# HGRN2 in a hybrid decoder layer on one core: state carried from tile to tile with decayed keys between chunks, and every projection step of a tile behind the next tile's scores

## The chip, the core and the metric

The kernel runs on one core of a Trainium2 chip. The core has five engines that run side by side, each with its own queue of instructions: TensorE (PE) for matmuls, VectorE (DVE), ScalarE (ACT), GpSimd (POOL), and SyncE (SP), which here only issues transfers. They wait for each other through semaphores. The metric is the time of one execution on the device in microseconds (us); lower is better.

## The reference, cut to what matters

A layer normalizes x (1024 tokens by 1024 channels, float32), projects it with one matrix into the inputs of four mixers (attention with forgetting, "FoX"; a state-space scan, "SSD"; gated linear attention, "GLA"; and HGRN2, "HGRN"), then adds cross-attention and a gated feed-forward part. The change touches HGRN alone. It has 4 heads with keys of 64 and values of 64 channels, and runs causally over time in chunks of 16 tokens:

```
q_dec = q * exp(g_cs)                 # g_cs: cumulated log decay inside the chunk
k_inv = k * exp(-g_cs)
k_end = k * exp(g_cs[:, :, -1:] - g_cs)
att = where(causal, einsum('bnihd,bnjhd->bnhij', q_dec, k_inv), 0.0)
o = einsum('bnhij,bnjhv->bnihv', att, v)
d_state = einsum('bnjhd,bnjhv->bnhdv', k_end, v)
s_in = scan_chunk_states(d_state, exp(g_cs[:, :, -1])[..., None])     # s * g + ds
o = o + einsum('bnihd,bnhdv->bnihv', q_dec, s_in)
```

Every chunk so has its own state s_in, 64 x 64 for a head, and the states follow one from another: 64 chunks in a row.

## The kernel before

All four mixers stand in `mixers_block`, with every engine's program written out by hand; the order of the work is the order of the code. Data lie with channels on the 128 partitions and the 1024 tokens along the row (a "slot"; `data(s)` is a slot, `tile(s, i)` the 128 tokens of tile i). So a pair p of heads fills the partitions, and there are two pairs.

**The projection runs in the gaps of the mixers.** Its unit is a half: one group of 128 columns of w_in against 512 tokens, 8 steps in k with three matmuls each (a high and a low part of both factors, `split_matmuls`, lines 99 to 101), 24 matmuls. ACT makes the high part of a group's weights (`hi`, L449), DVE the low part (`lo`, L759), and ACT copies each finished half out of PSUM (`copy_out`, L461). `fill(s0, s1)` issues single steps on PE, `halves(m0, m1)` whole halves. The table `_HG` says which halves stand beside HGRN: two in each of the four stretches of the preparation (`HG_PREP`), one at each of tiles 0 to 3, none at tiles 4 to 7 (`HG_TILE`).

**Preparation.** For each pair DVE and ACT in turn make the decays over all 1024 tokens (lines 565 to 576 on ACT, 830 to 849 on DVE): q_dec in `data(B + p)`, k_inv in `data(A + 4 + p)`, k_end in `data(B + 2 + p)`. The last one counts `h_prep`; PE, POOL and DVE wait for it before the tiles.

**Tiles.** A tile is 128 tokens, 8 chunks. On PE `hgrn_scores(i)` transposes values and k_end (L1169) and makes the scores of all four heads, k_inv against QX (L1175; QX is q_dec with the other head's rows set to zero, made by POOL, L407). DVE copies the scores through the mask M16, which keeps only what is causal and within one chunk (L856). `hgrn_states(i, p)` makes the eight d_state of each head in one matmul with 512 columns (L1184); for that POOL spreads the values over eight blocks (VX, L414). DVE then forms the eight states of a pair one after another, `S * ED + d_state`, one instruction of 64 x 64 for each head and chunk (L870), 32 for a tile. `hgrn_outputs(i, p)` needs all eight: two matmuls of masked scores with the values (L1196), then eight with 16 columns, each with its own chunk's state (L1199). ACT copies the transposes (L581) and the outputs (L585).

After tile 7 PE waits until every half is copied out and goes on with the norms of FoX (L1120), whose squares ACT makes first (L501).

## Time and profile before

| | |
|---|---|
| median of 3 runs | 1805.25 us (1805.08 to 1807.98) |
| the profiled execution, its own time | 1803.33 us |
| its span, first to last instruction | 1801.6 us |
| PE busy | 1690.7 us, 94% of the span |
| DVE, ACT, POOL busy | 876.9, 666.7, 74.3 us |
| mean granted TensorE clock | 0.974 of full speed |
| preparation, first projection step to first tile | about 137 to 184 us |
| tiles of HGRN | about 184 to 305 us |

Instructions are named by their line, engine and operation, then output and inputs, shapes, count, and time. A float32 matmul leaves two records on PE (a transpose leaves one), so 32 matmuls read as x64. Matmuls overlap: the distance between two starts is the price of one in a row, the duration shown is longer. "PEld" is the load of the factor that stays in the array; its columns are the second number in 128*64. A clock of 1.00 is TensorE's 2.4 GHz, 0.50 its 1.2 GHz.

### The profile page before, as it was taken

Reading aid. Unit: us, or ns where it says so; the run is one execution under the profiler, and the core shown is the slowest. Engines: PE = TensorE matmul, PEld = TensorE weight load, DVE = VectorE, ACT = ScalarE, POOL = GpSimd, SP = SyncE. Lnnn points to the kernel's source line nnn. Section 1 sums busy time; section 2 is a strip of 40 time slices with the busy share of each in tenths; the row PEclk is TensorE's granted clock in tenths of the full one; section 3 lists DMA queues with packets and bytes.
Section 4 is the critical chain, followed back from the end, with each engine's and each line's share of the span. In section 5 each row is a group of like instructions: output and inputs, shape, how many; then the busy total and the mean of one; then the engine's idle time right before and its main releaser. Section 6 shows DMA issues by size and latency. Waiting matters only on the chain.

```text
span 1801.6 us, 20927 instructions
## 1 busy us (share of the span) xinstructions
PE 1690.7 (94%) x8140; PEld 1350.6 (75%) x8140; DVE 876.9 (49%) x1471; ACT 666.7 (37%) x1186; POOL 74.3 (4%) x119
## 2 busy tenths in 40 slices
PE   6999898999887786999999999999999999999997
PEld 5788565666665454878888888888888888888886
DVE  4315576567466564544345325555533455555322
ACT  5224112754522435434343214334333344433321
POOL 2000432000010020000000000000000000000000
PEclk9999898999999898999999999999999999999999
DMA  5121000000020212600001113333222333333222
GB/s 143 47 48 37 23 12 1 24 24 25 24 70 13 70 59 67 243 6 24 1 24 65 36 47 94 94 103 96 72 92 94 118 101 103 113 94 105 88 97 97
DMA packets 166922, 121.32 MB, mean 67 GB/s; under 512 B 23448, under 2 KB 140456, under 8 KB 166824
## 3 DMA queue, kind: packets, MB, share of 16 engines
q1 hardware_dynamic: 165496, 115.53, 21.3%
q10 hardware_dynamic: 1328, 4.46, 0.7%
q8 instruction: 65, 1.06, 0.2%
q14 instruction: 33, 0.27, 0.0%
HBM read 115.77 MB, written 4.19 MB: 67 GB/s over the span
## 4 chain that ended last, share of the span: by engine, by line
PE 59%; DVE 1%; ACT 0%; DMA 0%; issue 0%; DVEq 0%
PE tail_b L99 18%; PE tail_b L100 18%; PE tail_b L101 18%; PE tail_b L2119 2%; PE tail_b L2094 1%; PE tail_b L2083 0%; PE tail_b L2106 0%; PE tail_b L2031 0%; DVE tail_wl L1795 0%; PE tail_b L2154 0%; PE tail_b L2238 0%; DMA tail_wr<-in_w_out 0%; DVE tail_xs L1830 0%; ACT tail_xs L1630 0%; DVE XR L1958 0%
## 5 line engine op out<-in xcount | busy, mean ns | idle before, releaser
L1951 DVE TENSOR_TENSOR ff_wl<-ff_wr,ff_wh 128x512 fp32r<-128x512 f32 (+1 forms) x176 | 168.5, 958 | 329.8 <-ACT ff_wh L1738 329.8
L1738 ACT ACTIVATE ff_wh<-ff_wr 128x512 fp32r<-128x512 f32 (+1 forms) x176 | 149.0, 847 | 377.6 <-PE tail_b L101 377.6
L99 PE MATMUL tail_b<-HH,ff_wh 128*128 128x512 f32 x704 | 273.9, 389 | 0.0
L100 PE MATMUL tail_b<-HL,ff_wh 128*128 128x512 f32 x704 | 273.9, 389 | 0.0
L101 PE MATMUL tail_b<-HH,ff_wl 128*128 128x512 f32 x704 | 273.9, 389 | 0.0
L99 PE MATMUL mix_gb<-HH,mix_wh 128*128 128x512 f32 x432 | 180.2, 417 | 7.7 <-ACT slots L461 3.8
L100 PE MATMUL mix_gb<-HL,mix_wh 128*128 128x512 f32 x432 | 170.7, 395 | 0.0
L101 PE MATMUL mix_gb<-HH,mix_wl 128*128 128x512 f32 x432 | 170.5, 395 | 0.0
L99 PE MATMUL tail_b<-tail_wh,HH 128*128 128x512 f32 x384 | 153.9, 401 | 9.4 <-DVE tail_wl L1795 8.2
L99 PEld LDWEIGHTS tail_b<-HH,ff_wh 128*128 128x128 f32 x704 | 132.2, 188 | 27.6
L101 PEld LDWEIGHTS tail_b<-HH,ff_wl 128*128 128x128 f32 x704 | 132.2, 188 | 27.6
L100 PEld LDWEIGHTS tail_b<-HL,ff_wh 128*128 128x128 f32 x704 | 132.2, 188 | 27.1
L101 PE MATMUL tail_b<-tail_wh,HL 128*128 128x512 f32 x384 | 150.3, 391 | 0.0
L100 PE MATMUL tail_b<-tail_wl,HH 128*128 128x512 f32 x384 | 150.3, 391 | 0.0
L99 PEld LDWEIGHTS mix_gb<-HH,mix_wh 128*128 128x128 f32 x432 | 82.8, 192 | 31.8 <-issue 6.3
L759 DVE TENSOR_TENSOR mix_wl<-mix_wr,mix_wh 128x1024 fp32r<-128x1024 f32 x43 | 53.5, 1246 | 102.9 <-ACT mix_wh L449 102.6
L99 PE MATMUL tail_b<-ff_wh,ff_aha 128*128 128x512 f32 x256 | 100.2, 392 | 0.0
L100 PE MATMUL tail_b<-ff_wl,ff_aha 128*128 128x512 f32 x256 | 99.7, 389 | 0.0
L100 PEld LDWEIGHTS mix_gb<-HL,mix_wh 128*128 128x128 f32 x432 | 82.6, 191 | 18.8 <-issue 2.7
L101 PEld LDWEIGHTS mix_gb<-HH,mix_wl 128*128 128x128 f32 x432 | 82.5, 191 | 17.9
L99 PEld LDWEIGHTS tail_b<-tail_wh,HH 128*128 128x128 f32 x384 | 72.6, 189 | 24.3 <-issue 10.3
L101 PEld LDWEIGHTS tail_b<-tail_wh,HL 128*128 128x128 f32 x384 | 72.5, 189 | 15.6
(315 smaller groups left out, 2586.4 us busy)
## 6 DMA issues: line engine op xcount, KB each, us to landing
ff_wr<-in_ffn_w_up SPq DMA_DIRECT2D x88, 512.0 KB, 3.7
ff_wr<-in_ffn_w_down SPq DMA_DIRECT2D x88, 256.0 KB, 2.8
mix_wr<-in_w_in SPq DMA_DIRECT2D x26, 512.0 KB, 3.6
mix_wr<-in_xa_wkv SPq DMA_DIRECT2D x16, 512.0 KB, 3.6
XR<-in_x SPq DMA_DIRECT2D x8, 512.0 KB, 6.4
tail_wr<-in_w_out SPq DMA_DIRECT2D x16, 256.0 KB, 5.6
XR<-in_x ACTq DMA_DIRECT2D x1, 4096.0 KB, 19.2
tail_wr<-in_xa_wq SPq DMA_DIRECT2D x16, 256.0 KB, 4.4
```

Source lines behind the costliest of these rows:

```text
L99: pe.matmul(out, hi_w, hi_x, start=first, stop=False)
L100: pe.matmul(out, hi_w, lo_x, start=False, stop=False)
L101: return pe.matmul(out, lo_w, hi_x, start=False, stop=last)
L759: dve.tensor_tensor(WL[:, n % PART, :, :], WR[:, n % RAW, :, :], WH[:, n % PART, :, :], ALU.subtract)\
L1738: act.activation(part(FWH[m % FPART], m), part(FWR[m % FRAW], m), ACT.Copy).then_inc(w_hi, 1)
L1951: dve.tensor_tensor(part(FWL[m % FPART], m), part(FWR[m % FRAW], m), part(FWH[m % FPART], m), ALU.subtract)\
L2094: mm = pe.matmul(bank[3 + g][:, hh * N_MEM:(hh + 1) * N_MEM], QT[:, 2 * h + kk, :], ktr(2 * h + kk), start=(kk == 0), stop=(kk == 1))
L2119: mm = pe.matmul(bank3[6 + g][:, j, :], vv(m, d), PT[:, m, d // 2, :], start=(m == 0), stop=(m == 1))
```

## The change

The state is now kept per tile instead of per chunk, and what a chunk owes to earlier chunks of the same tile is computed as scores.

- **Scores.** The product within the chunk stays (now L1229 in the changed kernel). For each chunk a from 1 to 7 and each pair, PE multiplies the keys of chunks 0 to a-1, decayed up to the start of chunk a, by the two heads' queries of chunk a: 16a keys by 2 x 16 queries (L1234), 14 matmuls for a tile. They write where the first product left terms that are not wanted. The mask MC keeps all that is causal.
- **Keys.** DVE makes those keys from k_end and a table DECAY of decays between chunk ends (`hgrn_keys`, L882: for each pair one instruction of 256 elements a partition for a = 1 to 4, KLO, and one of 512 for a = 5 to 8, KHI). KHI's last block, keys decayed to the tile's end, is what is transposed for the state.
- **State.** One matmul of 128 columns for each pair (L1243) and four DVE instructions a tile (`hgrn_update`, L902) instead of 32. POOL's VX (L414 before) is gone.
- **Outputs.** Two matmuls of scores as before and one of 128 columns with the tile's state and QE, queries decayed from the tile's start, which POOL makes (L414 of the changed kernel). Outputs have a bank of their own (M[4]), scores two (M[1], M[5]), tile states two (M[2], M[3]).
- **Preparation.** For each pair DVE has a copy, a scan and a difference over 64 chunk ends, and a difference and a minimum over 512 elements for DECAY; ACT has two more exponentials (128 and 512 elements).
- **Projection.** `_HG` counts in steps: 16 in each stretch of the preparation (two halves, as before), and 4 in each of the eight tiles, all in `HG_B`, behind the outputs of tile i and the scores of tile i+1. `HG_A`, ahead of the outputs, is empty. The sum stays 4 halves.

```diff
-_HG = spread(2 * F0, 2 * S0, [2, 2, 2, 2] + [1, 1, 1, 1, 0, 0, 0, 0])
-HG_PREP, HG_TILE = _HG[:4], _HG[4:]
...
+_HG = spread(2 * F0 * KT, 2 * S0 * KT, [16] * 4 + [0, 4] * NT)
+HG_PREP, (HG_A, HG_B) = _HG[:4], in_two(_HG[4:])
...
-        work = SL[:, W1:W1 + 5, :].rearrange("p a b -> p (a b)")
-        VX = work[:, 0:2048].rearrange("p (h c d) -> p h c d", h=4, c=8)
-        S_HG = work[:, 2048:2048 + 2304].rearrange("p (q c e) -> p q c e", q=2, c=9)
+        work = SL[:, A:A + 4, :].rearrange("p a b -> p (a b)")
+        KLO = [[work[:, 768 * (2 * b + p):768 * (2 * b + p) + 256] for p in range(2)] for b in range(2)]
+        KHI = [[work[:, 768 * (2 * b + p) + 256:768 * (2 * b + p) + 768] for p in range(2)] for b in range(2)]
+        S_HG = [work[:, 3072 + 256 * b:3328 + 256 * b].rearrange("p (q e) -> p q e", q=2) for b in range(2)]
+        QE = [work[:, 3584 + 256 * b:3840 + 256 * b].rearrange("p (q t) -> p q t", q=2) for b in range(2)]
+        DECAY = [data(W1)[:, 512 * p:512 * p + 512] for p in range(2)]
+        EC, EX = [ED[:, p, 0:64] for p in range(2)], [ED[:, p, 64:128] for p in range(2)]
...
+                if i >= 2:
+                    pool.wait_ge(E("h_y"), i - 1)
+                for p in range(2):
+                    pool.tensor_tensor(QE[i % 2][:, p, :].rearrange("p (c j) -> p c j", j=CH_HGRN),
+                                       tile(B + p, i).rearrange("p (c j) -> p c j", j=CH_HGRN),
+                                       EX[p][:, 8 * i:8 * i + 8].unsqueeze(2).to_broadcast([P, 8, CH_HGRN]), ALU.mult)\
+                        .then_inc(E("h_qe"), 1)
...
+                act.wait_ge(E("hg_ends"), p + 1)
+                act.activation(ED[:, p, :], a1[:, 64:192], ACT.Exp).then_inc(E("hg_ed"), 1)
+                act.activation(DECAY[p], DECAY[p], ACT.Exp).then_inc(E("hg_ed"), 1)
+                halves(*begun(HG_PREP[2 * p + 1]))
...
+            hgrn_vk(0)
+            for i in range(NT):
+                if i + 1 < NT:
+                    hgrn_vk(i + 1)
+                new = range(*begun((HG_A[i][0], HG_B[i][1])))
+                act.wait_ge(E("h_y"), i + 1)
+                act.activation(MX[:, 6:8, i * P:(i + 1) * P], M3[4][:, 0:2, :], ACT.Copy).then_inc(E("h_yev"), 1)
+                for m in new:
+                    halves(m, m + 1)
+            act.wait_ge(E("h_yev"), NT)
...
+            dve.wait_ge(E("st_tr"), NT)
...
                 dve.wait_ge(E("hg_ln"), p + 1)
+                if p:
+                    dve.wait_ge(E("hg_ed"), 2 * p)
...
+                dve.wait_ge(E("hg_cum"), p + 1)
+                link(dve.tensor_copy(low, ends16(2)))
+                link(dve.tensor_tensor_scan(cum, SL[:, A + 3, PAD:PAD + 128:2], low, 0.0, ALU.mult, ALU.add))
+                by_tile = cum.rearrange("p (t c) -> p t c", c=8)
+                dve.tensor_tensor(before, cum, low, ALU.subtract).then_inc(E("hg_dif"), 1)
+                dve.tensor_tensor(DECAY[p].rearrange("p (t a b) -> p t a b", a=8, b=8),
+                                  by_tile.unsqueeze(3).to_broadcast([P, NT, 8, 8]),
+                                  by_tile.unsqueeze(2).to_broadcast([P, NT, 8, 8]), ALU.subtract).then_inc(E("hg_dif"), 1)
+                dve.wait_ge(E("hg_dif"), 2 * p + 2)
+                dve.tensor_scalar(DECAY[p], DECAY[p], 0.0, None, ALU.min).then_inc(E("hg_ends"), 1)
                 dve.wait_ge(E("hg_e1"), p + 1)
-                link(dve.tensor_copy(ED[:, p, :], SL[:, A, PAD + CH_HGRN - 1:SW:CH_HGRN]))
...
+            def hgrn_keys(i):
+                if i >= 2:
+                    dve.wait_ge(E("h_att"), i - 1)
+                    dve.wait_ge(E("h_tr"), i - 1)
+                for p in range(2):
+                    k = tile(B + 2 + p, i).rearrange("p (b j) -> p b j", j=CH_HGRN)
+                    decay = DECAY[p][:, 64 * i:64 * i + 64].rearrange("p (a b) -> p a b", b=8)
+                    for buf, a, nb in ((KLO[i % 2][p], 0, 4), (KHI[i % 2][p], 4, 8)):
+                        dve.tensor_tensor(buf.rearrange("p (a b j) -> p a b j", a=4, b=nb),
+                                          k[:, 0:nb, :].unsqueeze(1).to_broadcast([P, 4, nb, CH_HGRN]),
+                                          decay[:, a:a + 4, 0:nb].unsqueeze(3).to_broadcast([P, 4, nb, CH_HGRN]),
+                                          ALU.mult).then_inc(E("h_ka"), 1)
+
...
+                    dve.wait_ge(E("h_y"), i - 1)
+                dve.copy_predicated(ATT[i % 2], MC[:].bitcast(mybir.dt.uint32).unsqueeze(1).to_broadcast([P, 4, P]),
+                                    M3[1 + 4 * (i % 2)]).then_inc(E("h_am"), 1)
+
+            def hgrn_update(i):
+                dve.wait_ge(E("h_ds"), i + 1)
+                if i >= 1:
+                    dve.wait_ge(E("h_s"), 4 * i)
+                    dve.wait_ge(E("h_y"), i)
                 for p in range(2):
...
+                    for hh in range(2):
+                        q, e = slice(64 * hh, 64 * hh + 64), slice(64 * hh, 64 * hh + 64)
+                        dve.scalar_tensor_tensor(S_HG[(i + 1) % 2][q, p, e], S_HG[i % 2][q, p, e],
+                                                 EC[p][q, 8 * i + 7:8 * i + 8], M3[2 + i % 2][q, p, e], ALU.mult, ALU.add)\
+                           .then_inc(E("h_s"), 1)
+
+            hgrn_keys(0)
+            hgrn_keys(1)
+            dve.wait_ge(E("att_zero"), 1)
+            hgrn_mask(0)
+            dve.wait_ge(E("s_zero"), 1)
+            late = range(0)
+            for i in range(NT):
+                if i + 1 < NT:
+                    hgrn_update(i)
+                if i + 2 < NT:
+                    hgrn_keys(i + 2)
+                if i + 1 < NT:
+                    hgrn_mask(i + 1)
+                for m in late:
+                    halves(m, m + 1)
+                late = range(*begun((HG_A[i][0], HG_B[i][1])))
+            for m in late:
+                halves(m, m + 1)
...
+                    pe.transpose(M3[0][:, j, :], tile(B + 4 + j, i), ident)
+                pe.wait_ge(E("h_ka"), 4 * i + 4)
+                for j in range(2):
+                    last = pe.transpose(M3[0][:, 2 + j, :], KHI[i % 2][j][:, 3 * P:4 * P], ident)
+                last.then_inc(E("h_tr"), 1)
+
+            def hgrn_scores(i):
+                pe.wait_ge(E("h_qx"), 2 * i + 2)
                 if i >= 2:
-                    pe.wait_ge(E("h_yev"), i - 1)
-                for j in range(4):
-                    last = pe.transpose(M3[0][:, j, :], tile((B + 4, B + 5, B + 2, B + 3)[j], i), ident)
-                last.then_inc(E("h_tr"), 1)
-                pe.wait_ge(E("h_qx"), 2 * i + 2)
+                    pe.wait_ge(E("h_am"), i - 1)
+                att = M3[1 + 4 * (i % 2)]
+                for p in range(2):
+                    pe.matmul(att[:, 2 * p:2 * p + 2, :], tile(A + 4 + p, i), QX[:, 2 * p:2 * p + 2, :], start=True, stop=True,
+                              skip_group_check=True)
+                    for a in range(1, 8):
+                        keys, q = KLO[i % 2][p][:, 64 * (a - 1):64 * (a - 1) + 16 * a] if a <= 4 else \
+                            KHI[i % 2][p][:, P * (a - 5):P * (a - 5) + 16 * a], slice(16 * a, 16 * a + 16)
+                        mm = pe.matmul(att[0:16 * a, 2 * p:2 * p + 2, q], keys, QX[:, 2 * p:2 * p + 2, q], start=True,
+                                       stop=True, skip_group_check=True)
+                mm.then_inc(E("h_att"), 1)
...
+            def hgrn_states(i):
+                pe.wait_ge(E("h_vk"), i + 1)
+                if i >= 2:
+                    pe.wait_ge(E("h_s"), 4 * (i - 1))
+                for p in range(2):
+                    mm = pe.matmul(M3[2 + i % 2][:, p, :], VK[i % 2][:, 2 + p, :], VK[i % 2][:, p, :], start=True, stop=True)
+                mm.then_inc(E("h_ds"), 1)
+
...
+                vk, yb = VK[i % 2], M3[4]
+                pe.wait_ge(E("h_vk"), i + 1)
+                pe.wait_ge(E("h_am"), i + 1)
+                pe.wait_ge(E("h_qe"), 2 * i + 2)
+                pe.wait_ge(E("s_zero"), 1)
                 if i >= 1:
-                    pe.wait_ge(E("h_am"), i)
+                    pe.wait_ge(E("h_s"), 4 * i)
+                    pe.wait_ge(E("h_yev"), i)
...
+                    for hh in range(2):
+                        pe.matmul(yb[64 * hh:64 * hh + 64, p, :], vk[:, p, 64 * hh:64 * hh + 64], ATT[i % 2][:, 2 * p + hh, :],
+                                  start=True, stop=False, skip_group_check=True)
+                    mm = pe.matmul(yb[:, p, :], S_HG[i % 2][:, p, :], QE[i % 2][:, p, :], start=False, stop=True,
                                    skip_group_check=True)
                 mm.then_inc(E("h_y"), 1)
...
+            hgrn_transposes(0)
             hgrn_scores(0)
-            for p in range(2):
-                hgrn_states(0, p)
             for i in range(NT):
                 if i + 1 < NT:
+                    hgrn_transposes(i + 1)
+                    hgrn_states(i)
+                fill(*HG_A[i])
+                hgrn_outputs(i)
+                if i + 1 < NT:
                     hgrn_scores(i + 1)
-                halves(*HG_TILE[i])
-                for p in range(2):
-                    hgrn_outputs(i, p)
-                    if i + 1 < NT:
-                        hgrn_states(i + 1, p)
+                fill(*HG_B[i])
```

The first place is PE's own row of work for one tile. Here stands what it does before, from the transposes and scores of tile 3 to the first state matmul behind the outputs of tile 2 (gb is the projection, m0 holds transposes and outputs, m1 the scores, m2 to m5 the states; "..." stands for the other projection matmuls of the half):

```order
L1169 MATMUL mix_m0<-ident,slots 128x128 [waits mix_h_yev,mix_h_vk]
L1175 MATMUL mix_m1<-mix_scratch,slots 128x256 [waits mix_h_am,mix_h_qx]
L99 MATMUL mix_gb0<-HH,mix_wh 128x512 [waits mix_g_ev,mix_g_lo]
...
L1196 MATMUL mix_m0<-mix_scratch 64x128 [waits mix_h_vk,mix_h_yev,mix_h_s,mix_h_am]
L1199 MATMUL mix_m0<-slots 128x16 x8
L1184 MATMUL mix_m2<-slots,mix_scratch 128x512 [waits mix_h_s,mix_h_vx]
```

The like stretch of PE after the change, one tile earlier, from the transposes of tile 2 over the outputs of tile 1 and the scores of tile 2 to the first of the 12 projection matmuls:

```order
L1217 MATMUL mix_m0<-ident,slots 128x128 [waits mix_h_vk]
L1220 MATMUL mix_m0<-ident,slots 128x128 [waits mix_h_ka]
L1243 MATMUL mix_m3<-mix_scratch 128x128 [waits mix_h_vk]
L1257 MATMUL mix_m4<-mix_scratch 64x128 [waits mix_s_zero,mix_h_s,mix_h_qe,mix_h_yev,mix_h_am,mix_h_vk]
L1259 MATMUL mix_m4<-slots 128x128
L1229 MATMUL mix_m1<-mix_scratch,slots 128x256 [waits mix_h_am,mix_h_qx]
L1234 MATMUL mix_m1<-mix_scratch,slots 16x2x16
L1234 MATMUL mix_m1<-mix_scratch,slots 32x2x16
...
L1234 MATMUL mix_m1<-mix_scratch,slots 112x2x16
L99 MATMUL mix_gb0<-HH,mix_wh 128x512
```

The scores moved from ahead of the outputs to behind them, the projection from between scores and outputs to the tile's end, and the 512-column state matmuls became one of 128 columns ahead of the outputs.

The second place is DVE at the start of a tile's work, before (tile 1; M16 mask, then the chain of 64 x 64 updates, each with a wait for the one before it on the same head):

```order
L856 COPY_PREDICATED mix_scratch<-mix_m16,mix_m1 128x512 [waits mix_h_att]
L870 SCALAR_TENSOR_TENSOR slots<-slots,mix_ed,mix_m2 64x64 [waits mix_h_y,mix_h_ds]
L870 SCALAR_TENSOR_TENSOR slots<-slots,mix_ed,mix_m3 64x64
L870 SCALAR_TENSOR_TENSOR slots<-slots,mix_ed,mix_m2 64x64 [waits mix_h_s]
L870 SCALAR_TENSOR_TENSOR slots<-slots,mix_ed,mix_m3 64x64 [waits mix_h_s]
```

And DVE after the change, the mask of tile 0, the update of the state over tile 0, the keys of tile 2 and the mask of tile 1:

```order
L891 COPY_PREDICATED mix_scratch<-mix_mc,mix_m1 128x512 [waits mix_h_att,mix_att_zero]
L902 SCALAR_TENSOR_TENSOR slots<-slots,mix_ed,mix_m2 64x64 [waits mix_h_ds,mix_s_zero]
L902 SCALAR_TENSOR_TENSOR slots<-slots,mix_ed,mix_m2 64x64 x3
L882 TENSOR_TENSOR slots<-slots 128x256 [waits mix_h_tr,mix_h_att]
L882 TENSOR_TENSOR slots<-slots 128x512
L891 COPY_PREDICATED mix_scratch<-mix_mc,mix_m5 128x512 [waits mix_h_att]
```

The 32 updates with their waits became four, and four products for keys stand between update and mask (the two more that follow read the same and are left out).

## Rows read from the trace of the kernel before

**Rows 1.** Page, part 1: busy time and share of the span.

```profile
PE 1690.7 (94%) x8140; PEld 1350.6 (75%) x8140; DVE 876.9 (49%) x1471; ACT 666.7 (37%) x1186; POOL 74.3 (4%) x119
```

**Rows 2.** Page, part 4: the chain that ended last.

```profile
PE 59%; DVE 1%; ACT 0%; DMA 0%; issue 0%; DVEq 0%
```

**Rows 3.** Windows: length, then PE, PEld, DVE, ACT, POOL busy, clock, DMA.

```profile
137.00:184.00 47.00, 45.62 (x197) 37.31 (x196) 26.01 (x23) 21.59 (x26) 0.00 (x0) 0.96 0.20 45
184.00:306.00 122.00, 107.62 (x544) 74.91 (x544) 80.53 (x266) 12.56 (x24) 45.49 (x49) 0.90 0.04 9
```

**Rows 4.** Groups by shape, 184 to 306 us: busy, mean ns, idle before.

```profile
L870 DVE SCALAR_TENSOR_TENSOR slots<-slots,mix_ed,mix_m 64x64 f32<-64x64 f32 x256 | 71.7, 280 | 13.0 <-PE mix_m L1184 5.0
L414 POOL TENSOR_TENSOR slots<-mix_scratch,mix_cm 128x512 f32<-128x512 f32 x32 | 34.4, 1105 | 59.5 <-ACT mix_scratch L581 59.5
L1199 PEld LDWEIGHTS mix_m<-slots 128*128 128x128 f32 x256 | 31.5, 200 | 2.9 <-issue 2.9
L407 POOL TENSOR_TENSOR mix_scratch<-slots,mix_hm 128x256 f32<-128x256 f32 x16 | 9.5, 613 | 0.0
L856 DVE COPY_PREDICATED mix_scratch<-mix_m 128x512 f32<-128x512 uint32 x8 | 5.9, 732 | 5.7 <-PE mix_m L1175 5.5
L1196 PEld LDWEIGHTS mix_m<-mix_scratch 128*64 128x64 f32 x64 | 3.5, 139 | 20.7 <-issue 17.1 <-DVE mix_scratch L856 3.6
```

**Rows 5.** Timeline of PE, one tile: start, length, what, idle before; projection left out.

```profile
247.17 0.60 PE L1169 MATMUL mix_m<-ident,slots 128*128 128x128 f32 x4
247.61 1.03 PE L1175 MATMUL mix_m<-mix_scratch,slots 128*128 128x256 f32 x4
...
254.05 0.44 PE L1196 MATMUL mix_m<-mix_scratch 128*64 128x128 f32 x4
254.42 1.96 PE L1199 MATMUL mix_m<-slots 128*128 128x16 f32 x16
256.23 1.96 PE L1184 MATMUL mix_m<-slots,mix_scratch 128*128 128x512 f32 x4
...
262.10 0.60 PE L1169 MATMUL mix_m<-ident,slots 128*128 128x128 f32 x4
```

**Rows 6.** Timeline of PE: two projection matmuls, three starts apart.

```profile
249.17 0.40 PE L99 MATMUL mix_gb<-HH,mix_wh 128*128 128x512 f32 x1
...
249.86 0.40 PE L99 MATMUL mix_gb<-HH,mix_wh 128*128 128x512 f32 x1
```

**Rows 7.** Timeline of PE: first scores, last outputs, first norm of FoX.

```profile
187.23 2.08 PE L1175 MATMUL mix_m<-mix_scratch,slots 128*128 128x256 f32 x4 [2.58 <-POOL mix_scratch L407]
...
301.09 3.60 PE L1199 MATMUL mix_m<-slots 128*128 128x16 f32 x16
307.82 3.71 PE L1120 MATMUL mix_m<-slots,mix_bo 128*128 128x512 f32 x4 [3.14 <-ACT slots L501]
```

**Rows 8.** Timeline of DVE: scan, repeated operand, last of the preparation, low part.

```profile
149.87 2.29 DVE L838 TENSOR_TENSOR_SCAN slots<-slots 128x1024 f32<-128x1024 f32 x1
...
180.37 1.22 DVE L846 TENSOR_TENSOR slots<-slots 128x1024 f32<-128x1024 f32 x1
...
182.72 1.22 DVE L849 TENSOR_TENSOR slots<-slots 128x1024 f32<-128x1024 f32 x1 [1.13 <-ACT slots L576]
...
196.62 1.73 DVE L759 TENSOR_TENSOR mix_wl<-mix_wr,mix_wh 128x1024 fp32r<-128x1024 f32 x1 [6.45 <-ACT mix_wh L449]
```

**Rows 9.** Timeline of ACT in the preparation: two copies of halves.

```profile
154.11 0.57 ACT L461 ACTIVATE XR<-mix_gb 128x512 f32<-128x512 f32 x1
...
166.34 0.60 ACT L461 ACTIVATE XR<-mix_gb 128x512 f32<-128x512 f32 x1 [3.89 <-PE mix_gb L101]
```

**Rows 10.** Timeline of POOL: the four VX products of tile 1.

```profile
195.23 5.03 POOL L414 TENSOR_TENSOR slots<-mix_scratch,mix_cm 128x512 f32<-128x512 f32 x4 [2.91 <-ACT mix_scratch L581]
```

**Rows 11.** Timeline of PE in FoX: 32 records with 64 loaded columns.

```profile
405.42 1.92 PE L1271 MATMUL mix_m<-mix_scratch,slots 128*64 128x128 f32 x32
```

**Rows 12.** Windows of 1 us, columns as in rows 3.

```profile
271.00:272.00 1.00, 1.00 (x2) 0.38 (x2) 0.89 (x4) 0.15 (x1) 0.00 (x0) 0.50 0.00 0
```

More of the change, by code:

```diff
@@ L384, in _ @@
             keep(NEGK[:], ALU.is_ge, 0, [[1, P]], -1, NEG)
-            for m, ch in ((M64, CH_GLA), (M16, CH_HGRN)):
-                v = m[:].rearrange("p (c i) -> p c i", i=ch)
-                keep(m[:], ALU.is_ge, 0, [[1, P]], -1)
-                keep(v, ALU.is_ge, 0, [[-ch, P // ch], [0, ch]], 1)
+            keep(MC[:], ALU.is_ge, 0, [[1, P]], -1)
+            keep(M64[:], ALU.is_ge, 0, [[1, P]], -1)
+            keep(M64[:].rearrange("p (c i) -> p c i", i=CH_GLA), ALU.is_ge, 0, [[-CH_GLA, P // CH_GLA], [0, CH_GLA]], 1)
             for m, n in ((BM, 4), (BO64, 2)):
@@ L393, in _ @@
                 keep(v, ALU.is_ge, w - 1, [[w, n], [0, 64]], -1)
-            for m, n in ((HM4, 4), (HM2, 2), (CM8, 8)):
+            for m, n in ((HM4, 4), (HM2, 2)):
                 w = P // n
@@ L564, in _ @@
             for p in range(2):
-                halves(*HG_PREP[2 * p])
+                halves(*begun(HG_PREP[2 * p]))
                 act.wait_ge(E("hg_abs"), p + 1)
@@ L829, in _ @@
             link(dve.memset(SL[:, A + 3, PAD:SW:CH_HGRN], 0.0))
+            ends16 = lambda j: SL[:, A + j, PAD + CH_HGRN - 1:SW:CH_HGRN]
+            low, cum, before = a1[:, 0:64], a1[:, 64:128], a1[:, 128:192]
+            dve.wait_ge(E("st_tr"), NT)
             for p in range(2):
@@ L849, in _ @@
                 dve.tensor_tensor(z, z, a2, ALU.mult).then_inc(E("h_prep"), 1)
-            dve.wait_ge(E("att_zero"), 1)
-            dve.wait_ge(E("s_zero"), 1)
-            for i in range(NT):
+            dve.wait_ge(E("h_prep"), 2)
+            dve.wait_ge(E("hg_ed"), 4)
+            def hgrn_keys(i):
[10 more added lines that the diff above has]
+                                          ALU.mult).then_inc(E("h_ka"), 1)
@@ L853, in _, with hgrn_mask @@
+            def hgrn_mask(i):
                 dve.wait_ge(E("h_att"), i + 1)
                 if i >= 2:
[L855 to L873 removed]
```

87 lines of the change are left out of this document (14 added, 73 removed).

## The prediction

> **What bounds the kernel now.** First the page: PE is busy for 94% of the span [rows 1] and the chain that ended last is PE with hardly anything else [rows 2]. So only what PE does, or waits for, counts. Then the windows: the preparation of HGRN takes 47 us, of which PE works 45.6, and its tiles take 122 us, of which PE works 107.6 at a granted clock of 0.90 [rows 3]. Four halves of the projection stand in the tiles. One matmul of it costs 0.69 / 3 = 0.23 us [rows 6], a half 24 x 0.23 = 5.5, so 22 us of the 122 are projection. The other 100 are HGRN.
>
> The groups of that stretch [rows 4] show who makes PE wait: DVE updates states for 71.7 us, 256 instructions of 0.28 us one behind the other, and POOL spreads values for 34.4 us. The timeline of one tile [rows 5] shows PE's own bill, 262.10 - 247.17 = 14.9 us: transposes 0.44, scores and a half 6.44 (so 0.9 for the scores), outputs 0.37 + 1.81 twice, and what is left, 1.85 twice, states. Sixteen records with 16 moving columns cost 1.81 us, 0.113 each, though they move next to nothing; the load of 128 columns sets that price. A tile without a half costs PE 9.4 us, and DVE 32 x 0.28 + 0.73 = 9.7. Both bound the stage, taking turns.
>
> The stage runs from the first scores at 187.2 us to the last output at 301.09 + 3.60 = 304.7, and 3.1 us later the norms begin at 307.8 [rows 7].
>
> **The change part by part.** I add up where PE will stand, on the clock of the profiled execution.
>
> *Preparation.* For each pair DVE gets, behind the scan that ends at 152.2 [rows 8], three operations on 64 elements and two on 512. The nearest rows are 0.28 (64 x 64) and 0.73 us (512) [rows 4], so at most 2.3: done by 154.5. ACT, which began its copy at 154.1 [rows 9], now first has exponentials of 128 and 512 elements, some 0.3 and 0.6 (its 512-element copy takes 0.6 [rows 9]). So that copy slips by 0.8 (if short operations overlap) to 1.3 us; I take 1.0. The slip of the first pair is swallowed, since ACT later waits 3.9 us for PE anyway [rows 9]. That of the second moves the end of the preparation from 182.72 + 1.22 = 183.9 [rows 8] to 184.9. PE needs the slipped copy at about 166.3 - 2 x 5.5 = 155.4 and gets it at 155.7, so it may lose some tenths, twice; PE has 1.4 us to spare in this stretch (45.6 of 47 [rows 3]), which hides them. DVE's new wait on the transposes of the gates delays nothing: ACT takes up its result only after the next half.
>
> *First tile.* DVE then makes keys(0): two operations of 512 elements and two of 256. By 0.73 for 512 and 1.22 for 1024 [rows 4, 8] a 256 costs at most 0.5, so 2.5 us, until 187.4. POOL meanwhile zeroes less and makes QX (1.2 a pair of products [rows 4]). The trace shows that DVE and POOL collide: the low part of the weights took 1.73 us beside POOL's products, and those took 5.03 for four instead of the 34.4 / 32 x 4 = 4.3 of the mean [rows 8, 10]. By 0.5 us for a clash, one or two of them give 188.0 with bounds of 187.0 and 188.8; the first scores start at 188.3 with the last two transposes.
>
> The Trainium skill has a rule for this, and it speaks against the change ("SBUF — State Buffer", Who interferes with whom): a DVE instruction with two SBUF inputs and a GpSimd instruction that reads SBUF exclude each other for the whole instruction. The new keys are just that kind. By that rule in full the start would be 1 us later than by the row and each tile of DVE up to 2 us longer, which DVE has to spare (below); the sum by the rule would be 1 us higher.
>
> *Small score matmuls.* This is the unknown price: 14 matmuls a tile, 28 records, with 16 to 112 loaded columns and 32 moving. The nearest rows: 0.113 for 128 columns with 16 moving [rows 5], and 1.92 / 32 = 0.06 for 64 columns with 128 moving [rows 11]. The loads themselves read 200 ns for 128 columns and 139 for 64 [rows 4], so columns count. I take 0.06 up to 64 columns and 0.113 x columns / 128 above: for a pair 2 x (4 x 0.06 + 0.071 + 0.085 + 0.099) = 1.0, for a tile 2.0 us. The bounds are 448 / 128 x 0.113 x 4 = 1.6 and 28 x 0.113 = 3.2.
>
> The rule of the Trainium skill ("TensorE: Matmul & The Clock Gate", LDWEIGHTS (loading the stationary operand)) is that a load's time goes with its columns, at 1.2 columns a ns. That would make the 28 loads 1.5 us instead of my 2.0, and the whole kernel 4 us faster than my sum. The rows of the loads agree in direction, 139 ns for 64 columns against 200 for 128.
>
> *A tile in the steady state.* Transposes 0.44; two state matmuls of 128 columns, four records at 0.113, 0.45; outputs 2 x 0.37 [rows 5] + 4 x 0.113 = 1.19; scores 0.9 + 2.0 = 2.9; projection 12 x 0.23 = 2.76. Sum 7.74 us, against 14.9 with a half and 9.4 without. Is anything else as long? DVE: four updates 1.1, keys 2.5, mask 0.73, a low part (1.23 to 1.73) every second tile: 5.2, or 6 with clashes. POOL: 1.2 for QX and at most 1.2 for QE. ACT: two copies of 0.6 and every second tile a copy and a high part. The waits: mask(i) is ready 0.9 us after scores(i), and the outputs that need it stand 2.76 + 0.44 + 0.45 = 3.65 us behind, so the moved projection covers it. Without that cover PE would wait 0.9 - 0.9 = 0, behind transposes and states alone, plus some tenths of latency. The keys of tile i+2 are done 3.6 us after states(i), PE asks for them after 6.8. So PE runs through.
>
> *Sum.* Scores(0) run at the half clock, since PE stands idle ahead of them, as it did before (2.58 us right ahead of 187.2 [rows 7]): 2 x 2.9 = 5.8, from 188.3 to 194.1. Mask 0.9: 195.0. Outputs(0), scores(1), projection 6.85: 201.9. Tiles 1 to 6: 46.4, 248.3. Outputs(7) and projection 3.95: 252.2. Then the same 3.1 us until the norms: 255.3 instead of 307.8. That is 52.5 us less. Against the profiled execution's own 1803.33 this gives 1750.8; the median is 1.9 higher than that execution, so **1752.5, rounded to 1752 us**. Behind the norms nothing changes: no instruction of FoX, SSD, GLA or the tail is touched, and its transfers are short on a queue that is not waited for.
>
> **The rivals.**
>
> *The small matmuls cost the full load.* If 16 columns cost as much as 128, each tile has 1.2 us more and the first, cold one 2.4: 1762. For it: the price of 16 moving columns in [rows 5] did not fall with them. Against it: [rows 11].
>
> *The clock falls in every tile.* In the window at 271 the granted clock is 0.50 with PE busy all the time [rows 12], after outputs of 16 moving columns. A mean of 0.90 over 122 us [rows 3] means some 24 us at 0.50, 3 us a tile, and half of it lost. If each tile keeps that, 7 x 1.5 = 11 us: 1763. Against it: the new small records move 32 columns twice in 0.06 us and stand between wide ones, and 2.8 us of projection follow in each tile, where before a tile had none or a lump.
>
> *DVE becomes the bound.* If the keys, with three-level patterns and repeated elements, run at half rate, DVE's tile is 5.0 + 1.1 + 0.7 + 0.9 = 7.7, and with clashes 8.7: 6 to 7 us in all, 1758. Against it: L846, which also repeats an operand 16 times, takes the 1.22 us of L849 [rows 8].
>
> *Slower.* One mechanism: the small loads at the full price keep TensorE at 1.2 GHz through the whole stage, the projection steps being too short in one piece (2.8 us) to raise it. Then a tile costs 2 x (0.44 + 0.45 + 1.19 + 4.1 + 2.76) = 17.9, and the norms begin at 331: 1828 us. It turns to a loss when a tile takes more than (307.8 - 3.1 - 201.9 - 3.95) / 6 = 16.5 us. For it: the last outputs ran 3.6 us at 0.21 a record without a rise [rows 7]. Against it: the old tiles stood at 0.90 [rows 3] with a worse mix.
>
> *The change doesn't do what it says:* the stage keeps its length since something else held it, within 0.2% of 1805. Nothing in the rows speaks for it; PE's own bill alone was 9.4 a tile.
>
> **How the numbers follow.** My forecast 0.70, with an own range of 1744 to 1758 (small matmuls at 1.6: -3; a warm first tile: -3; the start's bounds and unseen gaps of 0.3 us a tile: +/-3). Full load 0.10, clock 0.10 (also both together, 1774), DVE 0.05, slower 0.03, nothing 0.02. The range 1743 to 1766 leaves out about 0.15. A measurement of this kernel tells 0.2% (3.6 us) from no change: faster 0.95, within 0.02, slower 0.03.
>
> **What would show it.** In the changed profile: the first transposes at about 185 and the norms at about 255; a period of 7.7 us from one tile's L1217 to the next; L1234 at some 2.0 us a tile; no wait of PE on the mask after tile 0; four L902 a tile and DVE idle for a quarter of it; the clock at 1.00 from tile 1 on. It is wrong if a tile's period is above 9, if L1217 waits for `h_ka`, or if a stretch at 0.50 comes back with each tile.

## The result, and the profile after

The changed kernel took 1764.16 us in the median of 4 runs (1762.33 to 1765.76), the kernel before 1805.82 beside it (4 runs, 1805.08 to 1807.98). The ratio is 0.9767, with a 95% interval of 0.9750 to 0.9784: 2.3% faster, 42 us. Predicted were 1752 us and a range of 1743 to 1766, so the time lies at the range's upper end. It lies outside the 1744 to 1758 that the prediction gave for its own mechanism alone; the wider range held because it took in two rivals, and neither of them happened (see below).

The page of the changed kernel, part 1, answers to [rows 1]:

```profile
PE 1662.3 (94%) x8104; PEld 1336.9 (76%) x8104; DVE 832.9 (47%) x1281; ACT 667.1 (38%) x1190; POOL 46.8 (3%) x99
```

The windows answer to [rows 3]; the first two are the stretches shown there, the next three lie in the first tiles, the last covers the steady ones:

```profile
137.00:184.00 47.00, 44.69 (x194) 35.82 (x193) 31.17 (x33) 22.65 (x29) 1.19 (x2) 1.00 0.20 46
184.00:306.00 122.00, 117.07 (x656) 85.11 (x656) 48.29 (x86) 46.51 (x80) 17.69 (x32) 0.90 0.07 18
...
186.00:188.00 2.00, 2.00 (x13) 1.22 (x11) 1.87 (x4) 0.60 (x1) 0.39 (x1) 0.50 0.03 8
202.00:204.00 2.00, 2.00 (x7) 1.62 (x7) 0.74 (x1) 0.00 (x0) 1.62 (x4) 0.50 0.00 0
204.00:206.00 2.00, 2.00 (x9) 1.66 (x8) 0.00 (x0) 0.00 (x0) 0.28 (x1) 0.83 0.00 0
206.00:257.00 51.00, 51.00 (x383) 39.31 (x382) 24.13 (x52) 8.29 (x16) 11.49 (x20) 1.00 0.08 22
```

The share of PE did not move, 94% before and after: it is the same bound with less on it. Between 186 and 204 us the clock is 0.50, although PE is busy without a gap; from 206 to 257 it is 1.00.

The timeline of PE answers to [rows 5] and [rows 7]. First what stands before and in tile 0, then one steady tile (of its transposes, its outputs and its 12 projection matmuls only the first rows), then the first norm:

```profile
182.81 0.44 PE L1217 MATMUL mix_m<-ident,slots 128*128 128x128 f32 x2 [1.48 <-DVE slots L870]
185.64 0.69 PE L1220 MATMUL mix_m<-ident,slots 128*128 128x128 f32 x2 [2.39 <-DVE slots L882]
186.12 1.06 PE L1229 MATMUL mix_m<-mix_scratch,slots 128*128 128x256 f32 x2
...
191.89 0.67 PE L1217 MATMUL mix_m<-ident,slots 128*128 128x128 f32 x2
...
202.10 0.77 PE L99 MATMUL mix_gb<-HH,mix_wh 128*128 128x512 f32 x1
...
206.13 0.38 PE L1217 MATMUL mix_m<-ident,slots 128*128 128x128 f32 x2
...
206.56 0.61 PE L1243 MATMUL mix_m<-mix_scratch 128*128 128x128 f32 x4
207.10 0.44 PE L1257 MATMUL mix_m<-mix_scratch 128*64 128x128 f32 x4
...
208.58 0.60 PE L1229 MATMUL mix_m<-mix_scratch,slots 128*128 128x256 f32 x2
209.11 1.24 PE L1234 MATMUL mix_m<-mix_scratch,slots 128*16 128x32 f32 x14
210.19 0.68 PE L1229 MATMUL mix_m<-mix_scratch,slots 128*128 128x256 f32 x2
210.79 1.24 PE L1234 MATMUL mix_m<-mix_scratch,slots 128*16 128x32 f32 x14
211.87 0.48 PE L99 MATMUL mix_gb<-HH,mix_wh 128*128 128x512 f32 x1
...
214.73 0.38 PE L1217 MATMUL mix_m<-ident,slots 128*128 128x128 f32 x2
...
265.01 1.82 PE L1170 MATMUL mix_m<-slots,mix_bo 128*128 128x512 f32 x3 [2.78 <-ACT slots L503]
```

A steady tile is the distance of two L1217: 214.73 - 206.13 = 8.60 us, and no row of it shows a wait. Tile 0 takes 206.13 - 191.89 = 14.24. The norms begin at 265.0 instead of 307.8, 42.8 us earlier; the profiled execution is 1764.18 against 1803.33, 39.2 us shorter. The 3.6 us between lie behind the norms, which the change does not touch. From the norms to the end of the span it takes 1801.6 - 307.8 = 1493.8 us before and 1762.5 - 265.0 = 1497.5 after, but with the old state in runs 1 and 2 below also 1497.2 and 1496.5. So it is scatter, and the kernel before was profiled in one of its quick executions; in medians the difference is 41.7 us.

### The profile page after: what moved, and what is told of

Same layout as the page of the kernel before. It is cut to its first block, busy times and chain, and to the rows that moved or that the text cites. A ratio compares the mean times of both kernels' runs of the same rounds, so it can differ in the third digit from the quotient of the medians.

```text
span 1762.5 us, 20610 instructions
## 1 busy us (share of the span) xinstructions
PE 1662.3 (94%) x8104; PEld 1336.9 (76%) x8104; DVE 832.9 (47%) x1281; ACT 667.1 (38%) x1190; POOL 46.8 (3%) x99
## 4 chain that ended last, share of the span: by engine, by line
PE 60%; DVE 1%; ACT 0%; DMA 0%; issue 0%; DVEq 0%
PE tail_b L99 18%; PE tail_b L101 18%; PE tail_b L100 18%; PE tail_b L2177 2%; PE tail_b L2152 1%; PE tail_b L2141 0%; PE tail_b L2164 0%; PE tail_b L2089 0%; DVE tail_wl L1853 0%; DMA tail_wr<-in_w_out 0%; PE tail_b L2212 0%; PE tail_b L2296 0%; DVE tail_xs L1888 0%; ACT tail_xs L1688 0%; DVE XR L2016 0%
```

## The experiments

All ratios are to the kernel before, run on the same chip. Two questions led: is it the state or the placing of the projection that pays, and what made the first tile and the steady tile longer than the sum.

**1. The placing alone, in the kernel before.** State per chunk as before, but four steps in each of the eight tiles.

```diff
-_HG = spread(2 * F0, 2 * S0, [2, 2, 2, 2] + [1, 1, 1, 1, 0, 0, 0, 0])
+_HG = spread(2 * F0 * KT, 2 * S0 * KT, [16] * 4 + [4] * NT)
...
-                halves(*HG_TILE[i])
+                fill(*HG_TILE[i])
```

The last is PE's line; ACT and DVE take `halves(*begun(HG_TILE[i]))`.

> The kernel before with only the projection table changed: 4 steps in each of the 8 tiles, at the old place between the scores of tile i+1 and the outputs of tile i. Theory (PE and DVE took turns as the bound, and lumps of a half left DVE idle): each tile costs PE 9.4 + 2.8 = 12.2 us against DVE's 10.7, so the stage from 187.2 to 304.7 us shrinks by some 8 to 14 us, to about 1793 to 1797. Rival (the placement gives nothing, all of the change's 42 us come from the state per tile): within 0.2% of before.

Measured: 1811.88 us, 1.0023 (1.0007 to 1.0039; 12 runs), not faster but slower by the little that can be told. The timelines of DVE and PE in tile 0 of this kernel say why:

```profile
196.35 1.73 DVE L759 TENSOR_TENSOR mix_wl<-mix_wr,mix_wh 128x1024 fp32r<-128x1024 f32 x1 [6.94 <-ACT mix_wh L449]
198.01 9.95 DVE L870 SCALAR_TENSOR_TENSOR slots<-slots,mix_ed,mix_m 64x64 f32<-64x64 f32 x32
...
203.07 0.69 PE L1196 MATMUL mix_m<-mix_scratch 128*64 128x128 f32 x4 [5.18 <-issue]
203.69 3.60 PE L1199 MATMUL mix_m<-slots 128*128 128x16 f32 x16
```

DVE waits 6.94 us for ACT's high part, and the 32 updates, which need nothing of it, stand behind. (ACT makes that part behind its copy of tile 1's transposes, for which it waits 8.8 us for PE. The kernel before has a like wait of 6.45 us [rows 8].) PE needs half of them (198.01 + 9.95 / 2 = 203.0) and goes on at 203.07, now with the clock down: the 16 records take 3.6 us instead of 1.96 [rows 5]. The two tiles with such a low part, 0 and 4, took 24.8 and 21.7 us, the others 12.2 to 12.6. My theory of a plain gain of 8 to 14 us fell.

**2. The same with DVE's low part behind the updates.**

```diff
-                halves(*begun(HG_TILE[i]))
                 for p in range(2):
...
                                .then_inc(E("h_s"), 1)
+                halves(*begun(HG_TILE[i]))
```

> e1_old_spread (the kernel before, 4 steps in each of 8 tiles) with DVE's low part of the weights behind the 32 state updates of a tile instead of ahead of them. Theory (e1 lost because that low part waits for ACT ahead of the updates, with 2.8 us of projection to cover it instead of 5.5: two waits of 5.2 us and a low clock behind them): the waits shrink to 2 or 3 us, and it is 8 to 14 us faster than before, ratio 0.992 to 0.996. Rival (the updates themselves are the wait): no better than e1, 1.002.

Measured: 1790.47 us, 0.9910 (0.9895 to 0.9924). One line of DVE's program at another place, which acts twice beside the tiles, is worth 1.1%, 20 us. In DVE's timeline the updates now come first and the low part meets no wait:

```profile
190.67 9.97 DVE L869 SCALAR_TENSOR_TENSOR slots<-slots,mix_ed,mix_m 64x64 f32<-64x64 f32 x32 [2.07 <-PE mix_m L1184]
200.67 1.23 DVE L759 TENSOR_TENSOR mix_wl<-mix_wr,mix_wh 128x1024 fp32r<-128x1024 f32 x1
201.93 0.73 DVE L856 COPY_PREDICATED mix_scratch<-mix_m 128x512 f32<-128x512 uint32 x1
```

From tile 2 on a tile takes 12.2 us, which is PE's own work, 9.4 + 2.8; tiles 0 and 1 take 13.6 and 12.8, with the clock at 0.50 for some 3 us. So the old structure, placed like this, had 0.9% of the 2.3%. Whether filling the idle time ahead of its first scores, as run 8 does below for the changed kernel, would give it more was not tried.

**3 and 4. Other places in the changed kernel.** Once all steps ahead of the outputs, once whole halves ahead of the outputs of tiles 0 to 3 and none later, which is the distribution of before.

```diff
-_HG = spread(2 * F0 * KT, 2 * S0 * KT, [16] * 4 + [0, 4] * NT)
+_HG = spread(2 * F0 * KT, 2 * S0 * KT, [16] * 4 + [4, 0] * NT)
...
+_HG = spread(2 * F0 * KT, 2 * S0 * KT, [16] * 4 + [8, 0] * 4 + [0, 0] * 4)
```

> The changed kernel with the 4 steps of each tile ahead of the outputs and not behind the next scores. Theory (in the steady state PE never waits, so the place inside a tile is worth nothing; the steps of tile 0 come earlier and raise the clock sooner): 0 to 4 us faster than the changed kernel's 1764. Rival (the steps must stand behind the scores to cover the mask): PE waits about 1 us a tile, 1770 to 1773.

> The changed kernel with the old table: a whole half ahead of the outputs in tiles 0 to 3, none in tiles 4 to 7. Theory (same work on PE, only tenths of waits where the cover is gone: mask ready 0.9 us after the scores, transposes and states cover 1.0): 1760 to 1766. Rival (the cover is needed): tiles 4 to 7 wait 1 us or more each and the clock falls in them, 1770 or more.

Measured: 1762.21 us, 0.9746 (0.9728 to 0.9763), with tiles of 8.53 us; and 1762.74 us, 0.9754 (0.9738 to 0.9769), with tiles of 11.25 us with a half (one took 12.6, since PE waited 1.0 us for a low part of DVE) and 5.8 to 6.0 without. Neither differs from the change itself (0.9767, and 0.9760 repeated) by what can be told. So with the state per tile neither the cover for the mask nor the spreading was needed: the placing that the change also makes is worth nothing that can be told against these two. Transposes and states alone cover the mask. Only where they are missing too, ahead of the outputs of tile 7, does PE wait, 0.86 us in run 4.

**5. All steps behind tile 7.**

```diff
+_HG = spread(2 * F0 * KT, 2 * S0 * KT, [16] * 4 + [0, 0] * 7 + [0, 32])
```

> The changed kernel with all 32 steps behind the outputs of tile 7. Same work on PE. Theory (only the projection raises the granted clock; the profile of the changed kernel shows 16 us of tile work at 0.50 until the first projection step): the tiles stay at 1.2 GHz throughout, 11.5 us each instead of 5.7, and the kernel is at 1790 to 1810, about as slow as before the change. Rival (the clock rises by itself in the tiles' mix of matmuls): 1760 to 1772.

Measured: 1792.35 us, 0.9911 (0.9894 to 0.9929), 28 us slower than the change. The windows of this kernel, two at 0.50 and the one in which it rises:

```profile
194.00:204.00 10.00, 10.00 (x53) 7.33 (x52) 3.67 (x10) 0.98 (x2) 1.69 (x5) 0.50 0.00 0
234.00:244.00 10.00, 10.00 (x53) 7.33 (x52) 3.81 (x9) 0.98 (x2) 1.90 (x4) 0.50 0.01 2
248.00:252.00 4.00, 4.00 (x32) 2.57 (x28) 1.67 (x4) 0.38 (x1) 0.00 (x0) 0.77 0.00 0
```

PE is busy for 10.00 of 10 us and stays at 0.50 for some 60 us, with five tiles of 10.21 us in a row; then, at about 250 us, the clock rises in the midst of the same work, for which the trace shows no cause. I had expected it to stay down throughout. This execution was the quickest of the five, the others took 6 to 7 us longer, so in them the rise may have come later; they have no trace. Here placing does pay, through the clock: tiles without projection, entered at 1.2 GHz, did not bring it up for 60 us.

**6 and 7. The price of the small matmuls.** Once every one of them loads 128 columns, once they are left out.

```diff
-                        keys, q = KLO[i % 2][p][:, 64 * (a - 1):64 * (a - 1) + 16 * a] if a <= 4 else \
-                            KHI[i % 2][p][:, P * (a - 5):P * (a - 5) + 16 * a], slice(16 * a, 16 * a + 16)
-                        mm = pe.matmul(att[0:16 * a, 2 * p:2 * p + 2, q], keys, QX[:, 2 * p:2 * p + 2, q], start=True,
+                        keys, q = KHI[i % 2][p][:, P * (a % 3):P * (a % 3) + P], slice(16 * a, 16 * a + 16)
+                        mm = pe.matmul(att[:, 2 * p:2 * p + 2, q], keys, QX[:, 2 * p:2 * p + 2, q], start=True,
```

In the other the loop `for a in range(1, 8)` with its matmul is gone. Neither kernel computes the layer: the first has wrong keys in these products, the second leaves out the scores between the chunks of a tile.

> The changed kernel with every small score matmul loading 128 columns of keys instead of 16 to 112 (wrong keys; the scores come out as other numbers). Theory (the price is set by the loaded columns, 0.113 us a record at 128): 14 records go from 1.08 us to 1.6, two sets a tile, 8 tiles, the first two of them at half the clock: 8 to 11 us slower than the changed kernel, about 1773. Rival (the price is set per instruction, not by columns): no change.

> The changed kernel without the 14 small score matmuls of each tile (the scores between chunks of a tile are left as the first product wrote them, so the output is not the reference's); the keys are still made. Theory (PE bound in every tile): 2.16 us less a tile, 6 at full clock, 2 at half: 13.0 + 7.2 = 20 us faster, about 1744, with DVE (5 to 6 us a tile) still below PE's 6.4. Rival (DVE or a wait takes over at once): less than 10 us faster.

Measured: 1769.28 us, 0.9788 (0.9772 to 0.9803), and 1734.94 us, 0.9603 (0.9585 to 0.9620). The timeline of PE in the first of them, the records of one pair and what follows:

```profile
215.70 1.64 PE L1233 MATMUL mix_m<-mix_scratch,slots 128*128 128x32 f32 x14
217.18 0.68 PE L1229 MATMUL mix_m<-mix_scratch,slots 128*128 128x256 f32 x2
```

Fourteen records with 128 loaded columns cost 217.18 - 215.70 = 1.48 us, 0.106 each, the same 14 in the changed kernel 210.19 - 209.11 = 1.08, 0.077 each. A tile grows from 8.60 to 9.22 us, and the kernel by 4 to 5 us in all. The trace is plainer than the ratio, whose interval overlaps that of the changed kernel; and this execution also had 3.4 us at the half clock in tile 5 (see the last section). I had expected 8 to 11 us: with 0.113 a record two sets would have cost 1.0 us more a tile, and they cost 0.62. Without them a tile takes 6.06 us: they cost 2.54 where they stand, 0.4 more than their own 2.16. And the kernel is 29 us faster, where I had expected 20. The norms start at 238.68 instead of 265.01, 26.3 us earlier: six steady tiles give 6 x 2.54 = 15.2, and the stretch at 0.50, in which two sets of them stood, gives the rest. The scores of tile 0 are done at 188.3 instead of 191.9, and tile 0 takes 195.04 - 188.34 = 6.7 us instead of 14.24: 3.6 + 7.5 = 11.1 us. Four sets of 14 records at the half clock cost 4 x 1.82 = 7.3 of these 11.1; the rest comes from the clock, which rises much sooner. The windows of this kernel:

```profile
188.00:190.00 2.00, 2.00 (x12) 1.68 (x12) 1.12 (x2) 0.56 (x1) 1.37 (x3) 0.60 0.00 0
190.00:192.00 2.00, 2.00 (x16) 1.49 (x16) 1.75 (x6) 0.42 (x3) 0.54 (x2) 1.00 0.00 0
```

Without the small matmuls the clock is back at 1.00 at 189.6 us, 3.4 us after the last transposes ahead of the first scores began, and 2.5 us ahead of the first projection matmul (192.09). With them it stood at 0.50 for 19 us of such work. So it is the small matmuls that held it down in the changed kernel.

**8. Projection steps ahead of the first scores.** Eight of the 32 steps run between preparation and tile 0, three stay in each tile.

```diff
+_HG = spread(2 * F0 * KT, 2 * S0 * KT, [16] * 4 + [8] + [0, 3] * NT)
+HG_PREP, HG_START, (HG_A, HG_B) = _HG[:4], _HG[4], in_two(_HG[5:])
...
+            halves(*begun(HG_START))
...
+            fill(*HG_START)
             pe.wait_ge(E("h_prep"), 2)
```

The line with `halves` stands on ACT ahead of its work for tile 0 and on DVE behind `hgrn_keys(1)`.

> The changed kernel with 8 of the 32 steps moved into PE's idle time between the preparation (last step at 181.2 us) and the first scores (186.1), and 3 steps in each tile instead of 4. Theory (4.4 us of idle time are filled, and the clock never falls, so the tile work from 186 to 206 us takes 12 us instead of 20): 11 to 13 us faster than the changed kernel, about 1752. Rival (the clock's low stretch has another cause than the idle time and stays): 4 us faster, about 1760.

Measured: 1751.59 us, 0.9683 (0.9669 to 0.9697), 12 to 15 us faster than the change, where 11 to 13 had been expected. PE's idle time ahead of the scores is gone, and in its timeline the first scores cost what steady ones do:

```profile
188.82 0.38 PE L1221 MATMUL mix_m<-ident,slots 128*128 128x128 f32 x2
...
189.25 0.60 PE L1233 MATMUL mix_m<-mix_scratch,slots 128*128 128x256 f32 x2
189.78 1.24 PE L1238 MATMUL mix_m<-mix_scratch,slots 128*16 128x32 f32 x14
...
192.54 0.42 PE L1221 MATMUL mix_m<-ident,slots 128*128 128x128 f32 x2
```

**9. Only tile 0's steps ahead of its outputs.**

```diff
+_HG = spread(2 * F0 * KT, 2 * S0 * KT, [16] * 4 + [4, 0] + [0, 4] * 7)
```

> The changed kernel with only tile 0's 4 steps moved ahead of its outputs. Theory (the projection is what raises the clock, so scores(1) and the outputs after it run at 2.4 GHz): 2 to 4 us faster than the changed kernel, and the profile shows scores(1) in 3.3 instead of 5.8 us. Rival (any matmul raises it after a while): no change.

Measured: 1760.21 us, 0.9737 (0.9724 to 0.9750), some 3 to 5 us less than the change, with intervals that just touch (and overlap that of run 12, the change repeated). The trace is plain where the ratio is not. From its second step on the projection runs at the full clock, and so do the scores of tile 1:

```profile
193.05 0.77 PE L99 MATMUL mix_gb<-HH,mix_wh 128*128 128x512 f32 x1
...
194.18 0.40 PE L99 MATMUL mix_gb<-HH,mix_wh 128*128 128x512 f32 x1
...
197.83 0.60 PE L1229 MATMUL mix_m<-mix_scratch,slots 128*128 128x256 f32 x2
...
201.12 0.41 PE L1217 MATMUL mix_m<-ident,slots 128*128 128x128 f32 x2
```

Scores(1) take 201.12 - 197.83 = 3.3 us here and 5.8 at the half clock.

**10. The warm start without any projection in the tiles.** The rival reading of run 5 was that such tiles are too light for 2.4 GHz; the other, that they keep the level which they find.

```diff
+_HG = spread(2 * F0 * KT, 2 * S0 * KT, [16] * 4 + [8] + [0, 0] * 7 + [0, 24])
```

> e7_warm_start with no projection step in the tiles and 24 behind tile 7; the clock is at 2.4 GHz when the tiles begin. Theory (the tiles' own matmuls can't raise the clock, but with no idle time between them they hold it): the same work, tiles of 5.7 us each at a clock of 1.00, ratio to before 0.968 to 0.970. Rival (the tiles' own matmuls let it fall): up to 5.7 us more for each tile that falls, ratio 0.975 to 0.99.

Measured: 1750.83 us, 0.9698 (0.9681 to 0.9715). One window over seven tiles of it:

```profile
189.00:229.00 40.00, 39.98 (x362) 30.29 (x360) 26.19 (x61) 6.97 (x14) 13.28 (x28) 1.00 0.05 14
```

The same tiles as in run 5, at 1.00 for 40 us, 5.82 us each instead of 10.21. The first reading falls. The second holds for these 40 us; that the level can also change in the midst of unbroken work is shown by run 5 itself, and by run 6 (last section).

**11. Run 8 with FoX's first squares ahead of ACT's last copy.** PE waits 2.78 us for them before the norms.

```diff
-            copy_out(2 * S0)
             act.preload_act_table_set(LN_EXP)
             squares(0)
             squares(1)
+            copy_out(2 * S0)
```

> e7_warm_start, and behind tile 7 ACT loads its table and makes the first two squares of FoX's norms before it copies out the last half, so that this runs beside the projection steps of tile 7 (3 steps, 2.1 us). Theory (the 2.9 us between the last step and the first norm are ACT's table load, copy and square in a row): PE waits 1 us instead of 2.9, so about 2 us faster than e7, ratio to the kernel before 0.967. Rival (the copy itself ends the wait either way): no change, 0.968.

Measured: 1749.02 us, 0.9685 (0.9667 to 0.9702). The wait falls to 1.33 us, as its timeline shows, and the releaser is another:

```profile
253.38 1.98 PE L1173 MATMUL mix_m<-slots,mix_bo 128*128 128x512 f32 x4 [1.33 <-ACT XR L463]
```

The norms start 1.2 us sooner than in run 8 (254.56 there), which is below what the ratios can tell. Runs 8, 10 and 11 are faster than both kernels.

**12. The changed kernel again.** No edit.

> The changed kernel unaltered, to have it on the same chip as the others. Both theories: 0.975 to 0.978 of the kernel before.

Measured: 1762.80 us, 0.9760 (0.9741 to 0.9779). The two medians of this kernel differ by 1.4 us, and its single executions spread from 1759.84 to 1766.53.

## Why the prediction was right, and where its sum was short

The mechanism was right: PE bounds the tiles, the state per tile takes work from it, and what is left runs without waits. The time came into the range in part by luck. The prediction's own mechanism had 1744 to 1758, and 1764 is outside of it; what took it in was the room left for two rivals, at 1762 and 1763, whose mechanisms the traces don't show. By the time alone one would have picked one of them. (The forecast itself is added up a little low: 1750.8 + 1.9 is 1752.7.)

The sum put the norms at 255.3 us; they start at 265.0. Its steps in order, with what they measured:

- **Start of the first scores: 188.3, measured 186.1 (-2.2).** The preparation's operations came as counted, 1.9 us on DVE where I had at most 2.3, and moved its end by 0.8 us against the scan of the first pair, where I had 1.0. The scan itself began 2.0 us sooner in this execution, whose clock was 1.00 in the preparation, not 0.96. That is scatter: in the timeline of PE of run 12, the same kernel at 0.96, the first scores start at the forecast's 188.3:

```profile
188.32 1.06 PE L1229 MATMUL mix_m<-mix_scratch,slots 128*128 128x256 f32 x2
...
194.08 0.67 PE L1217 MATMUL mix_m<-ident,slots 128*128 128x128 f32 x2
...
209.56 0.62 PE L1217 MATMUL mix_m<-ident,slots 128*128 128x128 f32 x2
```

  DVE and POOL did collide: in the timeline of POOL, tile 0 beside the keys and tile 1 alone,

```profile
183.31 1.73 POOL L409 TENSOR_TENSOR mix_scratch<-slots,mix_hm 128x256 f32<-128x256 f32 x2
185.00 1.39 POOL L414 TENSOR_TENSOR slots<-slots,mix_ed 128x128 f32<-128x128 f32 x2
...
192.16 1.18 POOL L409 TENSOR_TENSOR mix_scratch<-slots,mix_hm 128x256 f32<-128x256 f32 x2 [5.77 <-PE mix_m L1234]
193.30 0.76 POOL L414 TENSOR_TENSOR slots<-slots,mix_ed 128x128 f32<-128x128 f32 x2
```

  Both pairs took 0.55 to 0.63 us more beside the keys, and the eight keys 5.09 us, where the next four alone took 1.96. The price that I took for a clash, 0.5, was right. The Trainium skill ("SBUF — State Buffer", Who interferes with whom) calls what they share an exclusive lock. The rows agree that they hold each other up, but not that one stands still whenever the other works. As far as POOL's spans can be trusted, its four products took 3.08 us instead of 1.90, and DVE lost 5.09 - 2 x 1.96 = 1.17 us, so in those 3.08 us they did what takes 1.90 + 1.91 = 3.8 us alone.
- **Scores(0) at the half clock: 5.8, measured 191.89 - 186.12 = 5.77.** Right.
- **Mask, outputs(0), scores(1), projection: 7.8, measured 14.24 (+6.4).** This is the term that was mis-sized most, "Mask 0.9: 195.0. Outputs(0), scores(1), projection 6.85". I let the low clock end with scores(0). It lasted into the first projection steps, to 204.7 us, and everything between cost double. In run 12 it lasted to 210.0, and the same step took 209.56 - 194.08 = 15.48 us. Runs 8 and 9 take that stretch away or shorten it, and the time follows.
- **Tiles 1 to 6: 7.74 each, measured 8.60 (+5.2).** By parts: transposes 0.43 (0.44), states 0.54 (0.45), outputs 1.48 (1.19), wide scores 1.13 (0.9), small ones 2.16 (2.0), projection 2.86 (2.76). No term is far off, but all except the first are low, by 0.09 to 0.29 us. The likely cause, which no run takes by itself, is that a price from a long row of one kind (0.113 a record) lacks what a change of kind costs. My allowance for it, 0.3 a tile in the range, was a third of what came.
- **Outputs(7) and projection 4.35 (3.95), and then 2.93 (3.1) to the norms.** Close.

Together -2.2 + 6.4 + 5.2 + 0.4 - 0.2 = 9.6, the shortfall of 9.7.

*The price of the small matmuls.* I took 2.0 us a tile from rows, and it is 2.16. The groups by shape in the changed kernel's steady tiles, 206 to 257 us, show DVE's side and the loads by columns:

```profile
L882 DVE TENSOR_TENSOR slots<-slots 128x512 f32<-128x512 f32 x10 | 6.9, 686 | 0.0
L902 DVE SCALAR_TENSOR_TENSOR slots<-slots,mix_ed,mix_m 64x64 f32<-64x64 f32 x24 | 6.7, 279 | 16.5 <-PE mix_m L1243 16.0
...
L891 DVE COPY_PREDICATED mix_scratch<-mix_mc,mix_m 128x512 f32<-128x512 uint32 x6 | 4.5, 744 | 11.9 <-PE mix_m L1234 11.9
...
L882 DVE TENSOR_TENSOR slots<-slots 128x256 f32<-128x256 f32 x10 | 4.2, 423 | 0.2
...
L1234 PEld LDWEIGHTS mix_m<-mix_scratch,slots 128*112 128x112 f32 x24 | 3.3, 178 | 0.0
...
L1234 PEld LDWEIGHTS mix_m<-mix_scratch,slots 128*16 128x16 f32 x24 | 1.3, 94 | 4.0 <-issue 4.0
```

From 112 columns to 16 a load falls from 178 to 94 ns, 84 / 96 = 0.88 ns a column. The rate of the Trainium skill ("TensorE: Matmul & The Clock Gate", LDWEIGHTS (loading the stationary operand)), 1.2 columns a ns or 0.83 ns a column, agrees with that slope. Drawn on to zero columns the rows leave 80 ns on top of it, an estimate. By that rule alone the tile's small matmuls would have been 1.5 us, an estimate, too little by 0.7.

*The rivals.* Full load: no; run 6 is that case and costs 4 to 5 us more. The clock falls in every tile: no; it falls once, ahead of tile 0, and the window from 206 to 257 us shows 1.00. (Run 6 had one more fall, in tile 5.) DVE as the bound: no; in six steady tiles it waits for PE for 16.0 us ahead of the updates and 11.9 ahead of the masks, and the keys took 0.42 us for 256 and 0.69 for 512. Slower: its mechanism exists after all, in another place. Run 5 shows tiles of small matmuls that stay at 1.2 GHz for 60 us, but in the changed kernel the clock rose during the projection steps of tile 0 and then stayed up; I had given this 0.03, with tiles of 17.9 us, twice the steady tile of 8.60. Nothing changes: no.

*Which part pays.* Runs 3 and 4 against 1 and 2: the state per tile brings 2.3 to 2.5% with each of the three placings tried in the tiles, and the placing alone brings -0.2% or, with one line of DVE's program moved, 0.9%. Against that better placed old structure (0.9910) the state per tile is worth some 1.5%. The prediction did not part the two.
